# A gated linear attention stage: two chunks per call of key-value products, and two per call of outputs, alternating between halves of TensorE's array

## What is computed

```python
def gla_mixer(x, w_in, w_gate2, b_gate, g_norm, w_out):
    ...
    qc = to_chunks(q * (GLA_DK ** -0.5), GLA_DK)      # 4 chunks of 64 tokens, 4 heads, 128 keys
    kc = to_chunks(k, GLA_DK)
    vc = to_chunks(v, GLA_DV)                         # 256 values per head
    cum = jnp.cumsum(to_chunks(log_a, GLA_DK), axis=3)
    last = cum[:, :, :, -1:, :]
    k_dec = kc * jnp.exp(last - cum).astype(kc.dtype)
    chunk_decay = jnp.exp(last[:, :, :, 0, :])

    def step(state, inp):
        q_c, k_c, v_c, dec = inp
        state = dec[..., None] * state + jnp.einsum('bhck,bhcv->bhkv', k_c.astype(jnp.float32), v_c.astype(jnp.float32))
        o = jnp.einsum('bhck,bhkv->bhcv', q_c.astype(jnp.float32), state)
        return state, o
    ...
    o = rms_norm(o, g_norm.reshape(GLA_HEADS, GLA_DV)).reshape(B, S, GLA_HV)
    return (o * jax.nn.silu(r)) @ w_out
```

## Time and profile before

| | |
|---|---|
| Runs | 1584.51, 1585.82, 1586.26 us; median 1585.82 |
| The profiled execution | time 1586.33 us, span of the trace 1584.5 us |
| Mean granted TensorE clock | 0.96 of full speed |
| PE busy | 1483.4 us, 94% of the span |
| DVE busy / ACT busy | 533.6 us / 343.1 us |
| DMA | 462.36 MB, mean 292 GB/s |

### The profile page before, as it was taken

How to read it: one execution, slowest core, us unless ns; L and a number is a source line. 1 busy time by engine, 2 the same in 40 slices (tenths; PEclk the granted TensorE clock), 3 DMA queues, 4 the chain that set the end, 5 groups by cost and what they waited for, 6 DMA issues and landing times.

```text
span 1584.5 us, 16375 instructions
## 1 busy us (share of the span) xinstructions
PE 1483.4 (94%) x6884; PEld 851.7 (54%) x6884; DVE 533.6 (34%) x1034; ACT 343.1 (22%) x779; POOL 123.7 (8%) x57
## 2 busy tenths in 40 slices
PE   5999999999799999999989998999988998999995
PEld 2686884454378788455436444434335774444432
DVE  2582245421565124642151034121104354312113
ACT  3113231311211323131122023111102243201111
POOL 0007610000001900000000000000000000000000
PEclk8999999799899999989989998999998999899998
DMA  9986353899566641489946715999999421999995
GB/s 380 423 333 239 129 204 125 360 366 425 236 239 259 272 153 60 166 359 367 420 170 217 264 53 232 422 427 426 427 429 407 187 107 47 416 427 427 429 427 215
DMA packets 36395, 462.36 MB, mean 292 GB/s; under 512 B 3944, under 2 KB 6264, under 8 KB 7992
## 3 DMA queue, kind: packets, MB, share of 16 engines
q1 hardware_dynamic: 33824, 448.91, 69.2%
q0 software_dynamic: 1456, 10.18, 1.6%
q10 hardware_dynamic: 1032, 2.10, 0.7%
HBM read 458.03 MB, written 3.15 MB: 291 GB/s over the span
## 4 chain that ended last, share of the span: by engine, by line
PE 86%; DMA 7%; DVE 4%; ACT 1%; issue 1%; SPq 0%; DVEq 0%; ACTq 0%
PE work L729 18%; PE work L552 13%; PE work L781 10%; PE work L535 8%; PE acc L552 7%; DMA ring<-in_stream 5%; PE acc L535 5%; PE work L688 5%; PE acc L763 3%; PE work L544 3%; DMA early<-in_stream 2%; PE work L1216 2%; PE acc L1361 2%; PE work L1011 1%; PE work L746 1%
## 5 line engine op out<-in xcount | busy, mean ns | idle before, releaser
L729 PE MATMUL work<-ring,area 128*64 128x512 f32 x896 | 200.4, 594 | 5.9 <-DMA ring<-in_stream 5.8
L729 PEld LDWEIGHTS work<-ring,area 128*64 128x64 f32 x896 | 64.2, 137 | 131.4 <-issue 119.8
L552 PE MATMUL work<-ht_sb,ring 128*128 128x256 f32 x576 | 129.0, 384 | 0.0
L552 PEld LDWEIGHTS work<-ht_sb,ring 128*128 128x128 f32 x576 | 109.7, 192 | 18.5 <-issue 3.7
L2388 DVE SCALAR_TENSOR_TENSOR area<-area,comb_slot,work 128x256 f32<-128x256 f32 (+1 forms) x32 | 19.6, 614 | 285.7 <-ACT area L1623 285.7
L552 PE MATMUL acc<-ht_sb,ring 128*128 128x256 f32 x512 | 114.0, 381 | 0.0
L552 PEld LDWEIGHTS acc<-ht_sb,ring 128*128 128x128 f32 x512 | 96.1, 190 | 14.8 <-issue 2.0
L2400 DVE TENSOR_TENSOR area_r<-work,area_r 128x512 fp32r<-128x512 f32 x64 | 44.3, 692 | 176.6 <-ACT area_r L1631 143.6
L781 PE MATMUL work<-ring,area 128*64 128x512 f32 x384 | 91.6, 624 | 0.0
L729 PE MATMUL work<-area 128*64 128x512 f32 x384 | 86.7, 593 | 2.5 <-DMA area<-in_stream 2.5
L1623 ACT ACTIVATE area<-work 128x256 f32<-128x256 f32 (+1 forms) x32 | 15.7, 492 | 329.0 <-PE work L729 329.0
(11 more groups left out here) (331 smaller groups left out, 1957.0 us busy)
## 6 DMA issues: line engine op xcount, KB each, us to landing
ring<-in_stream SPq DMA_DIRECT2D x138, 2048.0 KB, 12.4
area<-in_stream SPq DMA_DIRECT2D x46, 2048.0 KB, 12.3
cst<-in_stream SPq DMA_DIRECT2D x14, 2048.0 KB, 17.4
early<-in_stream SPq DMA_DIRECT2D x14, 2048.0 KB, 22.7
ln_sb<-in_ln_vecs POOLq DMA_DIRECT2D x8, 1024.0 KB, 11.7
rel_rows<-mt_sb ACTq DMA_DIRECT2D x1, 2048.0 KB
cst<-in_consts POOLq DMA_DIRECT2D x1, 1209.0 KB, 16.0
x_sb<-in_x SPq DMA_DIRECT2D x1, 1024.0 KB, 15.0
```

The lines of the kernel that those rows point to most:

```text
L552: ins = pe.matmul(dst, w[:, k, c0:c0 + n], src[:, k0 + k, :], start=k == 0, stop=k == ks - 1)
L729: ins = pe.matmul(banks[half][e * CAP:(e + 1) * CAP, :], tokens[:, k, at:at + CAP], w[:, kk, e, half * W:(half + 1) * W], start=k == 0, st ...
```

## The change

`kv_chunks(t)` issues the products of the two chunks of one tile together: for each head first the chunk on partitions 0 to 63, then the one on 64 to 127. They go to different banks, the even chunk to `acc[0]`, `acc[1]` and the odd one to `acc[2]`, `acc[3]`. `o_chunks(t)` does the same with the outputs: for each head the even chunk on the columns that write partitions 0 to 63, then the odd one on those of 64 to 127. The second tile's outputs go to `acc[2]`, `acc[3]` and the first tile's to `acc[0]`, `acc[1]`. `grow` reads each chunk from its own pair of banks and waits for `kv_ready` by the pair. The numbers of matmuls and their shapes stay as they were. Behind line 1230 the changed kernel's line numbers are a few off.

```diff
-            def kv_chunk(c):
-                if c:
-                    pe.wait_ge(state_ready, c)
-                t, a = c // 2, CHUNK * (c % 2)
+            def kv_chunks(t):
+
+                if t:
+                    pe.wait_ge(state_ready, 2)
                 for h in range(GH):
-                    ins = pe.matmul(acc[h // 2][:, h % 2 * GDV:(h % 2 + 1) * GDV], GK[a:a + CHUNK, t, h * GDK:(h + 1) * GDK],
-                                    GV[a:a + CHUNK, t, h * GDV:(h + 1) * GDV], start=True, stop=True)
+                    for c in range(2):
+                        a = CHUNK * c
+                        ins = pe.matmul(acc[2 * c + h // 2][:, h % 2 * GDV:(h % 2 + 1) * GDV],
+                                        GK[a:a + CHUNK, t, h * GDK:(h + 1) * GDK],
+                                        GV[a:a + CHUNK, t, h * GDV:(h + 1) * GDV], start=True, stop=True)
                 ins.then_inc(kv_ready, 1)
 
-            def o_chunk(c):
-                pe.wait_ge(state_ready, c + 1)
-                if c >= 2:
-                    pe.wait_ge(o_taken, 1)
-                a = CHUNK * (c % 2)
+            def o_chunks(t):
+
+                pe.wait_ge(state_ready, 3 + t)
                 for h in range(GH):
-                    ins = pe.matmul(acc[2 + h // 2][a:a + CHUNK, h % 2 * GDV:(h % 2 + 1) * GDV],
-                                    GQT[:, h, c * CHUNK:(c + 1) * CHUNK], STATE[c][:, h, :], start=True, stop=True)
-                if c % 2:
-                    ins.then_inc(o_ready, 1)
+                    for c in range(2):
+                        a = CHUNK * c
+                        ins = pe.matmul(acc[2 * t + h // 2][a:a + CHUNK, h % 2 * GDV:(h % 2 + 1) * GDV],
+                                        GQT[:, h, t * P + a:t * P + a + CHUNK], STATE[2 * t + c][:, h, :],
+                                        start=True, stop=True)
+                ins.then_inc(o_ready, 1)
...
-            kv_chunk(0)
+            kv_chunks(0)
             job = begin()
             gate_half(5, 0, 0, job)
-            kv_chunk(1)
-            o_chunk(0)
+            kv_chunks(1)
             gate_half(5, 0, 1, job)
-            kv_chunk(2)
-            o_chunk(1)
+            o_chunks(0)
             job = begin()
             gate_half(4, 1, 0, job)
-            kv_chunk(3)
-            o_chunk(2)
+            o_chunks(1)
             gate_half(4, 1, 1, job)
-            o_chunk(3)
             job = begin()
             gate_half(5, 1, 0, job)
...
-                act.activation(XN[:, t, 0:W], acc[2][:, :], ACT.Copy)
-                act.activation(XN[:, t, W:D], acc[3][:, :], ACT.Copy).then_inc(o_taken, 1)
+                act.activation(XN[:, t, 0:W], acc[2 * t][:, :], ACT.Copy)
+                act.activation(XN[:, t, W:D], acc[2 * t + 1][:, :], ACT.Copy).then_inc(o_taken, 1)
...
-                dve.wait_ge(kv_ready, c + 1)
+                dve.wait_ge(kv_ready, c // 2 + 1)
                 if c:
                     dve.wait_ge(state_ready, c)
                 for h in range(GH):
-                    src = acc[h // 2][:, h % 2 * GDV:(h % 2 + 1) * GDV]
+                    src = acc[2 * (c % 2) + h // 2][:, h % 2 * GDV:(h % 2 + 1) * GDV]
```

## The result

The changed kernel takes 1575.71 us (median of 4 runs, 1575.31 to 1580.22) beside 1585.29 us for the kernel before in the same set: ratio 0.9943, 95% interval 0.993 to 0.9956. The mean over the 14 runs of the three sets is 1577.5 us, that of the 28 runs of the kernel before beside them 1585.5: 8.1 us less, 0.5%. The saving is small beside the whole program, so the chain of the changed stretch says more about its size than the total time does.

A forecast was written before the change was run, and what follows sets the result against it. PE was taken to bound the stretch: key-value calls save 3.84 us, output calls 3.74, shape changes 0.18, together 7.8; from the median, 1585.82 - 7.8 = 1578.0 us. The whole range was 1575.5 to 1581.0 us.

The forecast's parts named there:

- What bounds the kernel: First key-value call to transposes: the chain never leaves PE, so PE time saved there is saved from the chain.
- The pair's step: Key-value and output calls: two instructions on different array halves share one 0.215 us step; 16 instructions take 1.92 or 1.87 us.
- The lower bound: Changed stretch: if halves did not overlap at all, each call takes 1.72 us more and 0.9 us saving is left.
- The new wait: Second key-value call needs two DVE states; gate group hides it with 0.4 us to spare; 3.1 us if uncovered.
- The other margins: Outputs' products with the gate: first tile's ready at 916.8, 6.7 us early; second's by 923.3, due at 927.8.
- Downstream: Behind the stage: expert weight stream starts when PE is there, so it starts and ends 7.8 us earlier.
- the likeliest case: Whole kernel: the sum, 7.8 us saved, 1578.0 us, with 1576 to 1580.5 around it; 85%.
- Only the row halves gain: Output calls' column halves take turns or show weight loads; change worth 3.4 to 4.4 us, 1581.4 to 1582.4; 5%.
- No overlap: The four calls: halves don't overlap at all; 0.9 us saved, 1584.9 us; 3%.
- The second state's wait: Second key-value call waits for DVE's second state; costs up to 3.1 us, time 1578 to 1581; 3%.
- The time given back later: Weight stream bound by something that doesn't move, so the gain is lost there; 1585.8 us; 2%.
- A drain at each change between halves: Four calls: 28 changes between halves at 0.19 us each cost 5.3 us, only 0.9 saved; slower, 1590.2 us; 2%.

The follow-up runs named there:

- the three sets: Changed kernel, no further edit, timed three times beside the kernel before: 1575.71, 1578.1 and 1578.77 us; ratios 0.9943, 0.9952, 0.9946.
- paying the 7.76 us back: Changed kernel with its first key-value call lengthened by 36 pairs writing the same products again: 1585.34 us beside the kernel before's 1585.83, ratio 1.0.
- without cover: Changed kernel with the second key-value call directly behind the first, the gate group between them moved behind it: 1582.44 us in a single run.
- both repeats: Changed kernel timed twice again with no edit: 1578.1 us beside 1584.68 and 1578.77 beside 1586.22 for the kernel before.
- the two experiments with the output calls together: Changed kernel with both output calls behind one gate group: 1578.64 us; on top of that, last gate group ahead of the first transposes: 1576.73 us.
- one or both loops turned: Changed kernel, one chunk's heads all before the other's: both call kinds 1582.39 us; output calls only 1579.37; key-value calls only 1579.14.
- two heads at a time: Changed kernel with two heads of one half, then two of the other, in each call: 1579.48 us in a single run.

## Why the prediction was right, step by step

**What bounds the kernel.** Shown. PE's time in the stretch was the chain, and paying the 7.76 us back gave the old time, within 1.9 us.

**The pair's step.** 0.215 us predicted from the attention's and the experts' calls, 0.216 measured. Key-value calls 1.92 predicted, 1.93 measured; output calls 1.87, 1.88 measured; the gate groups 17.97, measured 3 x 3.63 + 7.06 = 17.95. The stretch: 25.55 predicted, 25.57 measured.

**The lower bound.** The prediction had the halves either alternate and overlap, or take turns at 0.9 us for the whole change. There is a state between: with the halves one after the other in the code the stretch saved 33.32 - 29.33 = 4.0 us. The bound of 0.9 us was not reached by any order that was tried.

**The new wait.** It was covered, with 0.3 us to spare where 0.4 us were predicted. Its price without cover was put at 3.1 us; it is 3.35 us and nearly as much again for the clock, 6.4 us. The prediction's term was the wait alone, without the low clock that came with it. It had no weight here, since the cover held.

**The other margins.** The first tile's product was to be ready 6.7 us early and the second 4.5. They were: DVE ended them at 916.97 and 923.45, for work due at 923.65 and 927.97. With both output calls together the first tile's came 3.4 us later, and no wait appeared in the chain.

**Downstream.** SP's issue came at 959.03, predicted 958.9 (timeline of SP's queue):

```profile
959.03 0.33 SPq L1474 DMA_DIRECT2D area<-in_stream  x1
```

That is 7.65 us earlier than before, since the changed stretch began 0.1 us later in this execution. Behind it the gain did not travel unchanged. In the profile of the changed kernel PE met a short stretch of low clock in the middle of the experts, which the kernel before did not have; windows and chain:

```profile
1022.20:1025.60 3.40, 3.40 (x11) 1.37 (x12) 0.33 (x2) 0.00 (x0) 0.00 (x0) 0.50 1.04 439
```

```profile
1022.67 8.50 PE work L781 x32
```

That group took 7.02 us before; 1.5 us were gone. No wait of PE explains the low clock: PE had been busy for all of the 10.1 us ahead of it (1012.0 to 1022.1), at 1.00. The 1.5 us came back where the weight stream sets the pace. The last slot of weights in the chain, from its issue to its landing, and the products that waited for it, in the changed kernel and then in the kernel before:

```profile
1139.67 34.56 DMA ring<-in_stream
...
1174.27 3.68 PE work L729 x16
```

```profile
1145.95 35.41 DMA ring<-in_stream
...
1181.40 3.68 PE work L729 x16
```

1181.40 - 1174.27 = 7.13 us, of 7.65 that SP's first issue had moved. PE itself stands only 1.24 us ahead of these products, in both. From 1130 us to here its waits for slots add up to 5.8 us in the changed kernel and 7.1 before: PE's loss went into them, and the stream set the pace in both. The same low stretch stands in the profiles of both repeats, at 1021.0 and 1020.9 us. It stands at 1021.7 and 1021.5 in the two experiments with the output calls together, and at 1027.9 without cover. It is missing where the time was paid back, in the experiments with one or both loops turned and in the one with two heads at a time, though the last is only 0.3 us behind the changed kernel. Why there and not here is left open.

**The time.** 1578.0 us predicted; the sets gave 1575.7, 1578.1 and 1578.8. The first of them lies below the 1576 to 1580.5 of the likeliest case and only 0.2 us inside the whole range. That it came out inside is luck of the scatter; that the other two lie within 0.8 us of the sum, and the stretch within 0.02, is not. The spread of 1 to 2 us was put down to the clock alone. The profiles name a second place: from SP's first issue at this stage to the last landing of the slot that ends the stage's stream it took 234.4 us in the kernel before (966.68 to 1201.1), 234.9 in the changed kernel (959.03 to 1193.9) and 233.4 in its first repeat (957.84 to 1191.2), a difference of 1.5 us between two executions of the same program.

**The rivals.** Only the row halves gain: refuted, column calls of 16 took 1.88 us with their loads inside. No overlap: refuted, the calls of 16 are as long as those of 8 were. The second state's wait: didn't occur. The time given back later: refuted, the last landing of the stream came 7.1 us earlier and the three sets are 6.6 to 9.6 us faster. A drain at each change between halves: refuted, 7 changes of half per call of 1.93 us cost nothing that shows.

## What to carry to other kernels

In the shapes of this kernel (float32, 256 columns) two matmuls that each use half of the array's rows or columns cost one, if both are free to start. Look for pairs that wait for each other only because they write the same PSUM bank, and give each its own; the column halves here share a bank, each writing its own 64 partitions, and overlap all the same. The two halves need not alternate strictly in the code: with four trace instructions of one half ahead they still start together, with eight the second half stands idle until four are through. Price an uncovered wait on PE at more than its length: here 3.35 us of standing cost 6.4 us with the low clock that came with it. And when a stage behind is bound by a stream that starts on PE's signal, a gain ahead of it can arrive nearly whole even if PE loses some of it within that stage: here 7.1 of 7.65 us did.

## What the runs showed of the hardware that was not expected

A matmul on one half of the array starts past four instructions of the other half that stand ahead of it in the program: the second half's first matmul began at the start of the first half's fifth, 0.97 us into the call on row halves, and 0.91 on column halves. A call is 12 steps for 16 instructions then.

Both output calls of one shape back to back save 0.35 us for two changes between array shapes.

While PE stood for 3.35 us the granted clock fell from the 2.4 to the 1.2 GHz level and stayed there for 6.8 us, 6.19 of them work of PE. Another low stretch, of 3.4 us, came in the changed kernel with PE busy without a break for the 10.1 us ahead of it; its cause is open.
